# Down projection of the FFN as seven half-size products, in one transformer-block kernel on one core

## The reference, cut to what matters

```
x = x + mx[2] * merge_branches(y_rnn_x, y_na_x, mrx, mnx, w_rnn_out, w_na_out, w_out)
x = x + mx[5] * conv_ffn(modulate(x, norm_ffn_g, mx[3], mx[4]), w_up, ffn_conv_w, ffn_conv_b, w_down)

def conv_ffn(xn, w_up, conv_w, conv_b, w_down):
    h = dwconv(xn @ w_up, conv_w, conv_b, FFN_CONV_LEFT)
    a, g = jnp.split(h, 2, axis=-1)
    return (jax.nn.silu(a) * g) @ w_down
```

## Time and profile before

| | us |
|---|---|
| median of 3 runs | 2162.35 |
| lowest and highest | 2161.12, 2162.81 |
| span of the profiled execution, first to last instruction | 2158.5 |
| median less span, what lies around the instructions | 3.85 |
| PE busy with matmuls | 2081.9 (96%) |
| DVE, ACT, POOL busy | 1573.5, 1058.9, 346.4 |
| DMA traffic | 209.92 MB |

### The profile page before, as it was taken

One profiled execution on the slowest core, in us unless ns is written; L12 is line 12 of the kernel. 1 busy time (PEld: TensorE's weight loads), 2 busy tenths in 40 slices (PEclk: granted clock), 3 DMA queues, 4 the chain that ended last, 5 costly groups with the idle time before them and its releaser, 6 DMA issues.

```text
span 2158.5 us, 28254 instructions
## 1 busy us (share of the span) xinstructions
PE 2081.9 (96%) x10750; PEld 1763.6 (82%) x10750; DVE 1573.5 (73%) x2780; ACT 1058.9 (49%) x1627; POOL 346.4 (16%) x234
## 2 busy tenths in 40 slices
PE   5999999999999999999998999999999999999999
PEld 1778888988888888888886788887888888888887
DVE  6688598585985967859859766668998888863433
ACT  3466665765766657666676420014444333433221
POOL 0031221221212221123023000000111111110000
PEclk9999999999999999999999999999999999999999
DMA  8421212012112120121202475362122221155552
GB/s 324 116 57 40 63 48 73 19 57 64 35 38 69 51 70 30 40 61 49 64 8 98 158 281 181 127 200 100 69 78 88 88 88 68 59 177 202 182 182 86
DMA packets 85687, 209.92 MB, mean 97 GB/s; under 512 B 24624, under 2 KB 30128, under 8 KB 85424
## 3 DMA queue, kind: packets, MB, share of 16 engines
q1 hardware_dynamic: 63360, 182.95, 24.6%
q0 software_dynamic: 5792, 20.97, 2.9%
q10 hardware_dynamic: 16400, 4.19, 0.9%
HBM read 171.39 MB, written 40.89 MB: 98 GB/s over the span
## 4 chain that ended last, share of the span: by engine, by line
PE 79%; DVE 11%; ACT 4%; issue 1%; DMA 1%; POOL 0%; SPq 0%; DVEq 0%; ACTq 0%; POOLq 0%
PE banks L47 14%; PE banks L46 14%; PE banks L45 14%; PE banks L986 4%; PE banks L857 4%; PE banks L2150 4%; PE banks L2152 4%; PE banks L2151 4%; PE banks L859 4%; PE banks L858 4%; PE banks L890 3%; DVE probT_low L1488 2%; PE banks L948 2%; DVE prob L1480 1%; PE banks L930 1%
## 5 line engine op out<-in xcount | busy, mean ns | idle before, releaser
L45 PE MATMUL banks<-qh,xnh 128*128 128x384 f32 (+1 forms) x640 | 223.1, 349 | 0.3 <-PEq L211 0.3
L857 PE MATMUL banks<-xnh,wh 128*128 128x512 f32 (+1 forms) x536 | 211.5, 395 | 4.4 <-ACT stage L1092 4.1
L47 PE MATMUL banks<-qh,xnl 128*128 128x384 f32 (+1 forms) x640 | 207.4, 324 | 0.0
L46 PE MATMUL banks<-ql,xnh 128*128 128x384 f32 (+1 forms) x640 | 207.3, 324 | 0.0
L859 PE MATMUL banks<-xnh,wl 128*128 128x512 f32 (+1 forms) x536 | 204.6, 382 | 0.0
L858 PE MATMUL banks<-xnl,wh 128*128 128x512 f32 (+1 forms) x536 | 204.4, 381 | 0.0
L1488 DVE TENSOR_TENSOR probT_low<-banks,probT_high 128x512 fp32r<-128x512 f32 (+2 forms) x256 | 138.9, 584 | 56.2 <-ACT probT_high L1160 55.1
L1160 ACT CAST probT_high<-banks 128x512 fp32r<-128x512 f32 (+2 forms) x256 | 117.1, 510 | 59.7 <-PE banks L948 50.8
L45 PE MATMUL banks<-yh,wh 128*128 128x512 f32 x372 | 145.2, 390 | 0.9 <-DVE wl L2337 0.9
L46 PE MATMUL banks<-yl,wh 128*128 128x512 f32 x372 | 145.1, 390 | 0.0
L47 PE MATMUL banks<-yh,wl 128*128 128x512 f32 x372 | 144.7, 389 | 0.0
(11 more groups left out here) (357 smaller groups left out, 5804.3 us busy)
## 6 DMA issues: line engine op xcount, KB each, us to landing
raw<-w_ff SPq DMA_DIRECT2D x33, 512.0 KB, 3.7
raw<-w_down SPq DMA_DIRECT2D x33, 512.0 KB, 4.4
raw<-w_fm SPq DMA_DIRECT2D x32, 512.0 KB, 6.7
raw<-w_qkv SPq DMA_DIRECT2D x24, 512.0 KB, 3.9
raw<-w_mix SPq DMA_DIRECT2D x24, 512.0 KB, 4.9
h_d<-conv_d SPq DMA_DIRECT2D x22, 512.0 KB, 2.6
sw_d<-h_d SPq DMA_DIRECT2D x44, 256.0 KB, 2.9
raw<-w_modT SPq DMA_DIRECT2D x16, 512.0 KB, 4.7
```

The source lines that it names most:

```text
L45: pe.matmul(out, w_hi(k), x_hi(k), start=(k == 0), stop=False)
L46: pe.matmul(out, w_hi(k), x_lo(k), start=False, stop=False)
L47: last = pe.matmul(out, w_lo(k), x_hi(k), start=False, stop=(k == chunks - 1))
L857: pe.matmul(out, fh[:, s, k, :], xnh[:, k, c0:c1], start=(k == 0), stop=False)
```

## The change

The down projection becomes Strassen's scheme over halves of the output rows, of the hidden chunks and of the tokens: seven products (`LEFT`, `RIGHT`, `SUM_2`, `SUM_3`, `SUM_1`, `CORNER`, `SUM_4`), each of 512 output rows by 11 hidden chunks (`HC`) by 512 tokens, so 77 steps with four row blocks each.

- Each step's operand is one raw slot of 128 x 1024, weights in its low half and tokens in its high half, split by one cast and one subtraction. Four raw slots and six operand slots are kept.
- Four of the products need sums of weight blocks. They are made in DRAM (`down_d`, four arrays of 11 x 128 x 512) by eight DMAs of POOL, four of them accumulating, at the end of mixer turns 1 to 6 (`down_sum`).
- Four products need sums of tokens. DVE makes them (`token_mix`) from `h_d` loads into four new slots `extras`, for `SUM_2` in place in `token_mixes`, else into the raw slot; during `LEFT` it makes the differences the others start from.
- Between products DVE combines banks (`combine`): 44 operations of 128 x 512 in all, and ACT copies four banks (`take`). The residual is loaded in 16 pieces `rests` and stored in 16 pieces.
- The last chunk's `h_d` store is issued by ACT in place of SP.

```diff
+            def down_sum(step):
+                if step:
+                    pool.wait_ge(down_sums, 16 * DOWN_SUMS[step - 1])
+                if step == 0:
+                    pool.dma_start(down_d[0], w_down[former, :, bottom_rows]).then_inc(down_sums, 16)
+                    pool.dma_start(down_d[2], w_down[former, :, top]).then_inc(down_sums, 16)
+                elif step == 1:
+                    pool.dma_start(down_d[0], w_down[latter, :, bottom_rows], accum_op=ALU.add).then_inc(down_sums, 16)
+                    pool.dma_start(down_d[2], w_down[former, :, bottom_rows], accum_op=ALU.add).then_inc(down_sums, 16)
...
+                if not first and not last:
+                    down_sum(i - 1)
...
+            def load_step(s):
+                p, k = divmod(s, HC)
+                if s >= 4:
+                    sp.wait_ge(down_lo, s - 3)
+                    if s - 4 < HC:
+                        sp.wait_ge(mixed, mix_count(s - 4))
...
+                sp.dma_start(raw_of(s)[:, low], weights_at).then_inc(raw_in[s % 4], 16)
+                if p in DIRECT:
...
+                    sp.dma_start(raw_of(s)[:, high], tokens_at).then_inc(raw_in[s % 4], 16)
+            def load_extra(s):
...
+                    if e >= 4:
+                        sp.wait_ge(mixed, e - 3)
...
+                    sp.dma_start(extra(e), src).then_inc(tokens_in[e % 4], 16)
...
+            for s in range(4, STEPS):
+                load_step(s)
+                load_extra(s)
+                if s == 6:
+                    sp.wait_ge(product, 7 * STRIPS)
+                if 6 <= s < 22:
+                    m, cols = place(s - 6)
+                    sp.dma_start(rest(s - 6), x1_d[m, :, cols]).then_inc(rest_in, 16)
...
+            def down(s, m):
+                p, k = divmod(s, HC)
+                hi, lo = down_slot(s)
+                out = every[:, (BANKS_A if p in ONTO_A else BANKS_D)[m], :]
+                pe.matmul(out, hi[:, m, :], line(hi)[:, high], start=(k == 0), stop=False)
+                pe.matmul(out, hi[:, m, :], line(lo)[:, high], start=False, stop=False)
+                return pe.matmul(out, lo[:, m, :], line(hi)[:, high], start=False, stop=(k == HC - 1))
...
+            for s in range(STEPS - DOWN_TAIL):
+                pe.wait_ge(down_lo, s + 1)
+                for m in range(4):
+                    if s % HC == 0:
+                        bank_free(s // HC, m)
+                    last = down(s, m)
...
+            for s in range(4, STEPS):
+                if s + 2 < STEPS and (s + 2) // HC != LEFT:
+                    token_mix(s + 2)
+                down_low(s)
+                if s // HC == LEFT:
+                    token_mix(s)
+                if s == 5:
+                    sum_conv(FC - 1, 1)
+                if s == 7:
+                    sum_conv(FC - 1, 0)
+                p, m = divmod(s - (DOWN_RING - 1), HC)
+                if p > RIGHT and m <= 4 and m >= 1:
+                    combine(p - 1, m - 1)
```

More of the change, by code:

```diff
@@ L1880 @@
 DOUBLES = 5
[L1881 removed]
 DOWN_RING = 6
 DOWN_TAIL = 4
+LEFT, RIGHT, SUM_2, SUM_3, SUM_1, CORNER, SUM_4 = range(7)
+STEPS = 7 * HC
+DIRECT = (LEFT, RIGHT, SUM_4)
+MIXED = (LEFT, SUM_2, SUM_3, SUM_1, CORNER)
+ONTO_A = (LEFT, SUM_2, SUM_1, SUM_4)
 ORDER_NORM = (0, 4, 1, 5, 2, 6, 3, 7)
[L1885 removed]
+BANKS_A, BANKS_D = (5, 4, 6, 7), (2, 0, 1, 3)
 def ffn_programs(nc, sem, sbuf, w_ff, w_down, ffn_p, mod, total, gain, ones, ident, eps, x1, ops, xh, xl, outT, x1_d,
[L1889 removed]
+                 h_d, down_d, down_sums, tokens_in, weights, every, merge_over, ffn_first):
     with ExitStack() as st:
@@ L1954, in op_source, with down_slot, slot_released, step_raw @@
             return (a, sw[:, :, :].rearrange("p a c -> p (a c)"), b, a[:, high])[g]
-        def down_slot(c):
+        def down_slot(s):
             return ((ops[:, 2, 0], ops[:, 2, 1]), (ops[:, 3, 0], ops[:, 3, 1]), (wh[:, 0], wl[:, 0]),
-                    (ops[:, 0, 0], ops[:, 0, 1]), (ops[:, 1, 0], ops[:, 1, 1]), (wh[:, 1], wl[:, 1]))[c % DOWN_RING]
+                    (ops[:, 0, 0], ops[:, 0, 1]), (ops[:, 1, 0], ops[:, 1, 1]), (wh[:, 1], wl[:, 1]))[s % DOWN_RING]
         DOWN_FREE = (7 * STRIPS - 7, 7 * STRIPS - 7, 7 * STRIPS - 5, 7 * STRIPS - 3, 7 * STRIPS - 1, 7 * STRIPS)
[L1962 to L1968, removed]
+        def slot_released(engine, s):
+            if s < DOWN_RING:
+                engine.wait_ge(product, DOWN_FREE[s])
+            elif (s - DOWN_RING) % HC == HC - 1:
+                engine.wait_ge(full, 4 * ((s - DOWN_RING) // HC + 1))
+            else:
+                engine.wait_ge(chunk_used, s - DOWN_RING + 1 - (s - DOWN_RING + 1) // HC)
+        def step_raw(s):
+            before = [n for n in range(s % 4, s + 1, 4)]
+            return FC // 2 * 16 + sum(32 if n // HC in DIRECT else 16 for n in before)
+        def mix_count(s):
+            return MIXED.index(s // HC) * HC + s % HC + 1
+        extra = lambda e: extras[:, e % 4, :]
+        mix = lambda k: token_mixes[:, k, :]
+        held = lambda n, m: full_c[:, m // 2, HALF * (m % 2):HALF * (m % 2) + HALF] if n else (tt, sw)[m // 2][:, m % 2, :]
+        rest = lambda r: rests[:, r, :]
+        gate = mod[:, 5 * KC:6 * KC, 0]
+        def place(r):
+            m = r % 4
+            return ((m, low), (4 + m, high), (4 + m, low), (m, high))[r // 4]
         def tr_place(step, n):
@@ L2043, in gpsimd @@
+            for r in range(8, 16):
+                store(r)
+            sp.wait_ge(stored, 16 * 16)
         def gpsimd(pool):
@@ L2588, in ffn_programs @@
+            for m in range(4):
+                combine(SUM_4, m)
         return sync, gpsimd, tensor, scalar, vector
```

295 lines of the change are left out of this document (177 added, 118 removed).

## The result

The changed kernel takes 2176.89 us (median of 4 runs, 2173.0 to 2180.21) against 2162.38 (2161.12 to 2162.81): a ratio of 1.0069, with a 95% interval of 1.0054 to 1.0083. It is slower by 0.5 to 0.8%, where 2135.5 was forecast. The profiled execution took 2177.34 us, its span 2175.5.

What follows compares the result with a forecast made beforehand. TensorE was taken to bound the kernel: span 2158.5 - 29.9 (removed matmuls) + 0 (start) + 2.0 (feed loop) + 1.0 (mixer) = 2131.6, plus 3.85 around the span, gives 2135.5 us; range 2131 to 2150.

Steps and rivals of the forecast that it cites:

- What came off TensorE: Down projection: 924 matmuls in place of 1056 at the same 0.2267 us each, 29.9 us less.
- Place three, the mixer: Mixer turns: POOL's eight DMAs of weight sums delay other work there; bounds 0 and 10 us, 1 taken.
- If sharing the engines doubled 4.9: Gate weights at a turn's start: landing time doubled from 4.9 us, TensorE waits 1.7 us in six turns, 10 us.
- most of the load is ahead of the burst: Gate weights' load: mostly done before the sums' DMAs, since POOL makes descriptors until about 373.5.
- All but one of those have tens of us: The new turn's loads beside the sums' DMAs: only the gate weights are tight, with 3.2 us in hand.
- The cover of POOL, 32.7 us: POOL's idle time in a turn, 9.21 and 23.52 us, covers issuing two sums' DMAs, 11.9 us.
- Place two, the feed loop: Down projection, steps 20 to 60: loop pace 2.78 us per step against TensorE's 2.72; stall 2.0 us, bounds 0 and 8.
- L: Feed loop: time from VectorE's end to the landing of the extra tokens, 3.4 to 3.9 us, taken as 3.6.
- 40 steps x (pace - 2.72) - 0.4: Feed loop's stall: pace is (L + 1.95) / 2, 0.4 us the reserve left after combining; 2.0 us at 2.78.
- Place one, the start: Down projection's first steps: VectorE has 18.4 us of work, 3 us in hand; bounds 0 and 3 us, 0 taken.
- the sums' DMAs hurt the mixer: Rival in the mixer: gate weights late in six turns, 10 us, or the roots: 2143.5 us; chance 0.13.
- The one on the slower side: Rival in the feed loop: token loads land as in a full queue, 4.8 us; stall 34 us: 2167; chance 0.04.

Runs made afterwards that it cites:

- e8: Changed kernel with the sums' DMAs ahead of a turn's last two sigmoids, plus extra token loads of steps 22 to 65 issued two steps earlier: 2132.18 us, ratio 0.9862.
- e4: Changed kernel with the store of a turn's last attention outputs issued ahead of the three 512 KB weight loads on SP: 2171.32 us, ratio 1.0044.
- e5: Changed kernel, where POOL waits for the next turn's gate weights to land before issuing the sums' DMAs: 2158.65 us, ratio 0.9991.
- e11: Changed kernel with the sums' DMAs issued behind the three bias sums, some 15 us into POOL's turn: 2139.99 us, ratio 0.9900.
- e12: Changed kernel with POOL waiting for gate weights before the sums' DMAs, and step 1's second accumulating DMA moved behind step 2's copy: 2152.3 us, ratio 0.9951.
- e2: Kernel before plus only the eight DMAs of the weight sums, which nothing reads; down projection untouched: 2198.5 us, ratio 1.0169.
- e7: Changed kernel with both DRAM-to-DRAM copies written as 1408 rows of 2 KB in place of 64 rows of 45 KB: 2167.55 us, ratio 1.0030.

## Why the prediction was wrong

**What came off TensorE: right.** 924 matmuls at the same pitch; e8's down projection is 211.9 us, with 209.5 of matmuls in it.

**Place three, the mixer: the step that failed.** I took 1 us with an upper bound of 10, and it was 36.7 at the start of the down projection. The bound failed, not only the choice in it: it priced one victim, the gate weights, and the runs show three (gate weights, the late store, POOL's bias sums beside VectorE). Four parts of its working:
- "If sharing the engines doubled 4.9": it did nearly that for the median (8.7). But in the turns with 45 KB rows it was 13.6, which costs 5.4 us, not 1.7. I knew these copies moved the same bytes and did not ask in what rows.
- "most of the load is ahead of the burst": it rested on POOL taking 5.9 us for 1408 rows, by proportion from the earlier trace rows. POOL took 1.06 and 0.88 us for the first two. The burst was there before the load.
- "All but one of those have tens of us": I did not list the stores. The 128 KB store for which ScalarE waits had next to nothing in hand: before, ScalarE already waited 2.4 us for it once. ScalarE's waits for it came to 28.6 us. With the store moved (e4) the turns of steps 0, 3 and 5 gave back 2.1, 1.5 and 5.7 of their 3.9, 2.6 and 9.8 us.
- The cover of POOL, 32.7 us, was right in size and wrong in kind. POOL was held 25.25 us, not 11.9, and the first piece of cover ends at the bias sums. Moved by 20 us they do not make the roots late (POOL still waited 9.23 us for VectorE before the next one); they meet VectorE.

None of the waits was priced with the half clock that follows the longer ones. With it, 25.3 us of waits became 37.5.

**Place two, the feed loop: mechanism right, size off.** Forecast 2.0 us of stall, bounds 0 and 8, at steps 61 to 66; measured 6.3 us in gaps over 0.3, 4.8 of them there. The extras landed 3.1 us after their own issue (2010 to 2100), 0.37 behind the weights' issue, so L was 3.5, near my 3.6. So it is the stall's formula, "40 steps x (pace - 2.72) - 0.4", that came out 4.3 us too small; whether by the pace or by the reserve of 0.4 these runs don't tell. The rule of the Trainium skill in the prediction ("DMA: Bandwidth & Descriptors", "Anatomy of one DMA") is stated for GpSimd's path, and these loads are SP's. Its estimate of 3.2 us, against the 3.5 measured, gave no stall at all; e8 shows that the stall was there and came from these landings. Waits and gaps of under 0.3 us, for which the sum had no term, took another 2.2 us of the down projection's 219.8.

**Place one, the start:** taken as 0, bounds 0 and 3; measured 1.8 us at steps 8 and 9, of which the second stands behind POOL's multiply, the 1.8 us that I had set against 3 us in hand. So those 3 us were not there; what had used them stays open.

**The sum.** Mixer +35.7, down projection 219.8 - 211.5 = +8.3: 2131.6 + 44.0 = 2175.6, the measured span within 0.1. That is bookkeeping: both terms are read from the same trace. The 3.85 us for what lies around the span compared the median of some executions with the span of another. Every execution on record with both numbers is 1.7 to 1.9 us longer than its own span, so this term was 2.0 us too large. Of the rivals, "the sums' DMAs hurt the mixer" named the cause and priced it at 10. The one on the slower side had the other mechanism (a full queue in the feed loop), which did not come. My chance of 0.04 for slower left out that the mixer's loss could exceed the gain. In size the 29.9 us of removed matmuls was right, and e8 shows it only once both stalls are out of the way: 2132.2 us. That this is near the forecast of 2135.5 says nothing for the forecast, which was made for the changed kernel.

## What to carry to other kernels

A DMA that nothing waits for is still work in a place. Before putting megabytes beside a tuned stage, list every load and store of that stretch with its time in hand, stores that free a buffer included, and put the burst where that list is empty: here the same eight DMAs cost 37 us at the turn's seam and nothing measurable some 50 us earlier or 15 us later. Bound such a cost by all transfers in the burst's way together, and add the half clock behind the longer waits (0.50 behind one of 5.37 us here). When a loop is at equal pace with the engine that it feeds, take the latency out of it rather than count on the average: one load issued two steps ahead was worth 8.3 us.

## What the runs showed of the hardware

- In all these runs an accumulating DMA from POOL, issued right behind another DMA of POOL with no wait of the program between them, went out only when that one had landed: held 25.25, 18.38 and 17.45 us behind an accumulating one (changed kernel, e5, e11), 10.90 behind a plain copy (e12). Two plain ones went out 1.06 us apart. The Trainium skill names another hold ("DMA: Bandwidth & Descriptors", "SWDGE vs HWDGE vs iDMA"), that VectorE keeps GpSimd from writing descriptors. The trace does not show it here: each hold ended within 0.4 us of the landing of the DMA ahead.
- A DMA of 1408 rows cost POOL 0.9 to 1.6 us, against 0.54 for 128 rows: far less than in proportion.
- From DRAM to DRAM 2816 KB took 11.0 (e11) to 14.1 us (e2) as 64 rows of 45 KB, 16.5 and 16.6 for the same two copies as rows of 2 KB (e7), and 18.2 to 27.0 accumulating (both in e7).
- Two operations of VectorE of 1.48 and 1.49 us took 4.37 and 5.20 beside POOL's bias sums (e5), and 1.48 and 1.49 beside the burst without them.
